# Three pads that move matmul operands by 64, 128 and 256 bytes in a one-core transformer kernel

## The chip, the cores and the metric

One Trainium2 chip, one of its cores. The metric is the device time of one launch in microseconds (us): the kernel is executed several times and the median stands for it.

## What is computed

The reference is two transformer blocks on 512 tokens of width 1024. What bears on the change are three large matrix products in the first block:

```python
q, k, v, z, gl = split_proj(h @ w_in[l])          # input products: h [512+256, 1024], w_in [1024, 7168]
...
act = gelu(einsum('td,thkd->thk', xb, u_tab[ib])) * gb     # PEER: 128 chosen experts of 16384 per token
out = einsum('thk,thkd->td', act, v_tab[ib])
```

The kernel computes the PEER part densely for three quarters of the tokens: the scores of all 16384 experts (keys `u`), a gate that is zero for those not chosen, and the sum over all values `v`. For the first 128 tokens it gathers the chosen rows instead.

## The kernel before

Every large product is done in split precision. An operand `a` of float32 is cut into `a_hi` (rounded to float32r by ScalarE) and `a_lo = a - a_hi` (VectorE or GpSimd), and a helper issues three matmuls of type float32r for each 128x128 block, at lines 100, 101 and 102:

```python
def product3(pe, out, left, right, start, stop):
    pe.matmul(out, left[0], right[0], start=start, stop=False)
    pe.matmul(out, left[0], right[1], start=False, stop=False)
    return pe.matmul(out, left[1], right[0], start=False, stop=stop)
```

The second argument of `pe.matmul` is the stationary operand (128 columns, loaded into the array by a LDWEIGHTS that the profile lists under PEld), the third the moving one (384 or 512 columns that stream through). In the profile's names the moving tile stands first and the stationary one second: `es_ob<-es_vh,es_ah` streams `es_vh` past `es_ah`. Each matmul has its own weight load, which runs while the matmul before it streams.

Three stages matter here, and in each TensorE follows one order without a break:

- Input products (`input_products`, `ip_` tiles, 57 to 477 us): 16 blocks of 512 output columns times 8 slices of the contraction. Stationary: token blocks of `ip_h_hi/lo` (later `ip_s_hi/lo`); moving: the weight slices `ip_wh`, `ip_wl` in a ring of 8. DMA brings a slice to `ip_raw`, ScalarE writes `ip_wh` (L652), GpSimd `ip_wl` (L728). 576 blocks, 1728 matmuls of 512 columns.
- Expert scores (`expert_scores`, `ex_` tiles, 855 to 1531 us): for each of 128 groups of keys and 8 slices, stationary `ex_uh`, `ex_ul` (made from `ex_u` by ScalarE L1559 and GpSimd L1684 or VectorE L1755), moving `wb_x_hi/lo`, 384 tokens. 3072 matmuls of 384 columns. `ex_u` is the same memory as `ex_room`, and is filled ahead of the stage.
- Expert sums (`expert_sums`, `es_` tiles, 1542 to 2069 us): for each of 128 groups of values, three token blocks by two halves. Stationary: the gated activations `es_ah`, `es_al` (made from `es_gated` at L2050, L2000, L2056); moving: the value rows `es_vh`, `es_vl`. 2304 matmuls of 512 columns.

Tiles are placed in SBUF in the order of their declaration, one behind the other, in each partition from byte 16,512 up. A tile in a `with` block of its own gives its room back, and a `hold` tile is never used: it only sets where the next one starts. Start bytes in a partition of the operands that this document speaks of, as the program places them (all strides inside these tiles are multiples of 512 bytes, so that the difference modulo 512 is the same for every matmul of a row):

| product | moving tile, start byte | stationary tile, start byte | moving minus stationary, modulo 512 |
|---|---|---|---|
| input products | ip_wh 147,584, ip_wl 163,968 | ip_h_hi 49,280, ip_h_lo 73,856 | 0 |
| expert scores | wb_x_hi 16,512, wb_x_lo 32,896 | ex_uh 149,632, ex_ul 166,016 | 0 |
| expert sums | es_vh 124,032, es_vl 140,416 | es_ah 162,944, es_al 169,088 | 0 |
| query product (mq, L100 to L102) | mq_ch 94,944, mq_cl 127,712 | wb_x_hi 16,512, wb_x_lo 32,896 | 96 |
| FFN up (pf_acc<-wb_x,pf_w) | wb_x_hi 16,512, wb_x_lo 32,896 | pf_wh 75,616, pf_wl 92,000 | 288 |
| FFN projection (pf_acc<-fo_p,wb_x) | fo_ph 165,728 / fo_pl 122,880 | wb_x_hi 16,512, wb_x_lo 32,896 | 224 for fo_ph, 384 for fo_pl |
| FFN down, half of the blocks (pf_acc<-pf_w,pf_h) | pf_wh 75,616, pf_wl 92,000 | pf_hh 120,672, pf_hl 165,728 | 0 |

Of the kernel before, what the change touches and what calls it, by code (L numbers as in the profile page):

```python
# [22 lines left out]
P = 128  # L23
# [11 lines left out]
KEPT_BASE = 102  # L35
LATENT_BASE = 106
DOWN_BASE = 215
DOWN_AT = 45600
SLICES_BASE = 205
GIVEN_BASE = 104  # L40
CARRIED_BASE = 200
# [34 lines left out]
def tensors(nc, ctx):  # L76
    def sb(name, shape, dt=F32):
        return ctx.enter_context(nc.sbuf_tensor(name, shape, dt, allow_name_mangling=True))

    def ps(name, shape, dt=F32):  # L80
        return ctx.enter_context(nc.psum_tensor(name, shape, dt, allow_name_mangling=True))

    return sb, ps
# [259 lines left out]
def input_products(nc, d, kept, kept_loaded):  # L343
# [17 lines left out]
    with phase(nc, "r0_loaded", "r1_loaded", "r2_loaded", "r3_loaded", "r4_loaded", "r5_loaded", "r6_loaded", "r7_loaded",  # L361
# [17 lines left out]
        sb, ps = tensors(nc, ctx)  # L379
# [15 lines left out]
            ada.append(early("ip_ada", [P, 2, KD, W]))  # L395
        z = sb("ip_z", [P, TT, 2 * D])
        raw = sb("ip_raw", [P, RING, W])
        wh = sb("ip_wh", [P, RING, W], F32R)
        wl = sb("ip_wl", [P, RING, W], F32R)
        stage = sb("ip_stage", [P, RING, W])  # L400
# [926 lines left out]
GR = 4  # L1327
GP = GT - 1
GI = 4
HOLD = 20736  # L1330
FIRST_BASE = 100
CARRIED_AT = 46688
GIVEN = KD * T + KD * 288 + 6 * KD + D
# [17 lines left out]
def expert_scores(nc, d, x, ut, ut_loaded, total, picked, weight, n_loaded, keyed, first):  # L1351
# [16 lines left out]
    with phase(nc, "u0_loaded", "u1_loaded", "u2_loaded", "u3_loaded", "u_hi", "u_lo", "h_done", "gelu_done",  # L1368
# [45 lines left out]
        sb, ps = tensors(nc, ctx)  # L1414
        hold = sb("ex_hold", [P, HOLD])
        uh = sb("ex_uh", [P, SLOTS, KD, NK], F32R)
# [451 lines left out]
def expert_sums(nc, d, total, picked, weight, n_loaded, keyed, ready, next_in, next_loaded, rows_stored):  # L1868
# [7 lines left out]
    with phase(nc, "e0_loaded", "e1_loaded", "v0_loaded", "v1_loaded", "v_hi", "v_lo", "gated", "act_hi", "act_lo", "key_done",  # L1876
# [5 lines left out]
        sb, ps = tensors(nc, ctx)  # L1882
        vt, ge, gk = keyed
        hold = sb("es_hold", [P, 2 * GI * (D + 2 * ND)])
        vh = sb("es_vh", [P, RING, D], F32R)
        vl = sb("es_vl", [P, RING, D], F32R)
        ag = sb("es_gated", [P, RING, ND])
        ah = sb("es_ah", [P, RING, ND], F32R)
        al = sb("es_al", [P, RING, ND], F32R)
# [1867 lines left out]
def whole_block(nc, d):  # L3757

    outer = ExitStack()
    with ExitStack() as ctx:  # L3760
        with ExitStack() as own:
            sb, _ = tensors(nc, own)
            given = (sb("ri_x", [P, KD, T]), sb("ri_low", [P, KD, 288]), sb("ri_mix", [P, 6, KD]), sb("jn_x0", [P, D]))
        with ExitStack() as own:
            sb, _ = tensors(nc, own)
            below = sb("wb_below", [P, 2 * KD * T])
            kept = (sb("at_q", [P, TT, D]), sb("at_k", [P, LK // P, D]), sb("at_ident", [P, P]))
        kept_loaded = [ctx.enter_context(nc.semaphore(f"{n}_kept", num=KEPT_BASE + i)) for i, n in enumerate(("keys", "queries"))]
        input_products(nc, d, kept, kept_loaded)
        x = split_pair(nc, ctx, "wb_x")  # L3770
        diff_attention(nc, d, x, kept, kept_loaded)
        with ExitStack() as own:
            sb, _ = tensors(nc, own)
            hold = sb("ex_before", [P, DOWN_AT - 2 * KD * T - 4128])
            keys_in = sb("ex_u", [P, 4, KD, NK])
        keys_loaded = ctx.enter_context(nc.semaphore("first_keys_loaded", num=DOWN_BASE))
        mix_and_query(nc, d, x, keys_in, keys_loaded)
        sb, _ = tensors(nc, ctx)
        total, picked, weight = sb("wb_po", [P, TT, D]), sb("wb_picked", [P, HK], U32), sb("wb_weight", [P, HK])
        with ExitStack() as own:  # L3780
            keyed = first_keys(nc, own)
        first = [ctx.enter_context(nc.semaphore(f"first_{n}_loaded", num=FIRST_BASE + i)) for i, n in enumerate(("gates", "values"))]
        given_loaded, rows_stored = [outer.enter_context(nc.semaphore(n, num=GIVEN_BASE + i)) for i, n in enumerate(("given_loaded", "x2_stored"))]
        expert_scores(nc, d, x, keys_in, keys_loaded, total, picked, weight, gather_semaphores(nc, ctx, "u", NR), keyed, first)
        expert_sums(nc, d, total, picked, weight, gather_semaphores(nc, ctx, "v", TT), keyed, first, given, given_loaded, rows_stored)
# [141 lines left out]
```

## Time and profile before

| | us |
|---|---|
| median of 3 runs | 3725.96 |
| lowest and highest run | 3718.17, 3726.2 |
| span of the profiled execution, first to last instruction | 3713.8 |
| TensorE busy in it | 3528.9 (95%) |
| VectorE / ScalarE / GpSimd busy | 2290.8 / 1476.7 / 1341.5 |

The profile gives its execution's own time as the span, 3713.8 us; the runs are timed from outside and lie 4.4 to 12.4 us above it. Matmuls are pipelined, and the duration that the profile gives one (389 ns for 512 columns) is longer than the time from its start to the next one's start. The rate of a stream of matmuls is therefore read in the timeline, from start to start; this distance is called the pitch here.

### The profile page before, as it was taken

How to read it: one execution, taken by the hardware profiler on the slowest of the kernel's cores; microseconds unless marked ns; L12 is line 12 of the kernel's file. 1: busy time of each engine (PE TensorE's matmuls, PEld its weight loads, DVE VectorE, ACT ScalarE, POOL GpSimd, SP SyncE). 2: the span in 40 equal slices, each digit the busy share in tenths (PEclk: the TensorE clock that was granted, in tenths of full speed). 3: DMA queues.
4: the chain of work that ended last, by engine and by line, in shares of the span. 5: the costliest groups of instructions: out<-in, count | busy, mean ns of one | idle time of the engine just before them, and what ended most of it. 6: DMA issues, size and time to landing. Idle time of an engine off the chain costs nothing. (4 is left out here: it accounts for less than half of the span.)

```text
span 3713.8 us, 58353 instructions
## 1 busy us (share of the span) xinstructions
PE 3528.9 (95%) x22109; PEld 2862.4 (77%) x22109; DVE 2290.8 (62%) x3622; ACT 1476.7 (40%) x2438; POOL 1341.5 (36%) x821
## 2 busy tenths in 40 slices
PE   8999988899998999899999899998999998989998
PEld 4777866788988999788888444897888864678887
DVE  5723167425999887688888866445566236646642
ACT  3312246334546996233333233223255214424540
POOL 3723400434776334454222011430334521413352
PEclk9999999999999999999999999999999997699999
DMA  7633410635678989999999335213333331032331
GB/s 273 228 101 113 168 48 1 238 128 168 220 224 274 323 318 342 361 369 364 357 349 360 105 115 169 80 32 119 90 100 91 113 132 69 1 115 81 100 113 57
DMA packets 367108, 651.14 MB, mean 175 GB/s; under 512 B 23944, under 2 KB 227592, under 8 KB 363716
## 3 DMA queue, kind: packets, MB, share of 16 engines
q1 hardware_dynamic: 321468, 475.37, 38.7%
q0 software_dynamic: 36864, 134.23, 9.7%
q10 hardware_dynamic: 8584, 38.89, 2.7%
q8 instruction: 132, 2.16, 0.2%
q14 instruction: 60, 0.49, 0.0%
HBM read 557.64 MB, written 96.00 MB: 176 GB/s over the span
## 5 line engine op out<-in xcount | busy, mean ns | idle before, releaser
L100 PE MATMUL ex_hb<-wb_x_hi,ex_uh 128*128 128x384 f32 x1024 | 350.8, 343 | 17.5 <-POOL ex_ul L1684 11.3
L101 PE MATMUL ex_hb<-wb_x_lo,ex_uh 128*128 128x384 f32 x1024 | 344.7, 337 | 0.0
L102 PE MATMUL ex_hb<-wb_x_hi,ex_ul 128*128 128x384 f32 x1024 | 344.5, 336 | 0.0
L100 PE MATMUL es_ob<-es_vh,es_ah 128*128 128x512 f32 x768 | 300.2, 391 | 11.8 <-DVE es_al L2056 11.8
L100 PE MATMUL pf_acc<-wb_x_hi,pf_wh 128*128 128x512 f32 (+2 forms) x768 | 298.3, 388 | 7.0 <-DVE wb_x_lo L2484 4.7
L101 PE MATMUL es_ob<-es_vl,es_ah 128*128 128x512 f32 x768 | 299.8, 390 | 0.0
L102 PE MATMUL es_ob<-es_vh,es_al 128*128 128x512 f32 x768 | 299.7, 390 | 0.0
L101 PE MATMUL pf_acc<-wb_x_lo,pf_wh 128*128 128x512 f32 (+2 forms) x768 | 297.7, 388 | 0.0
L102 PE MATMUL pf_acc<-wb_x_hi,pf_wl 128*128 128x512 f32 (+2 forms) x768 | 297.5, 387 | 0.0
L2035 POOL DMA_INDIRECT es_near<-in_peer_v,wb_picked x128 | 178.4, 1394 | 325.9 <-DVE wb_po L2059 320.6
L728 POOL TENSOR_TENSOR ip_wl<-ip_raw,ip_wh 128x512 fp32r<-128x512 f32 x128 | 190.8, 1499 | 226.8 <-ACT ip_wh L652 226.6
L1998 ACT ACTIVATE es_vh<-es_v 128x1024 fp32r<-128x1024 f32 x128 | 135.5, 1058 | 260.5 <-PE es_ob L102 170.7
L2054 DVE TENSOR_TENSOR es_vl<-es_v,es_vh 128x1024 fp32r<-128x1024 f32 x128 | 156.8, 1225 | 86.4 <-ACT es_vh L1998 86.3
L100 PEld LDWEIGHTS ex_hb<-wb_x_hi,ex_uh 128*128 128x128 f32 x1024 | 194.7, 190 | 19.7 <-POOL ex_ul L1684 12.5
L2519 DVE TENSOR_TENSOR pf_h<-pf_cv 128x512 f32<-128x512 f32 x44 | 174.5, 3965 | 50.3 <-ACT pf_cv L2395 50.2
L100 PE MATMUL ip_acc<-ip_wh,ip_h_hi 128*128 128x512 f32 x512 | 202.1, 395 | 0.9 <-DVE ip_s_lo L849 0.9
L101 PE MATMUL ip_acc<-ip_wl,ip_h_hi 128*128 128x512 f32 x512 | 201.3, 393 | 0.0
L102 PE MATMUL ip_acc<-ip_wh,ip_h_lo 128*128 128x512 f32 x512 | 201.1, 393 | 0.0
L652 ACT ACTIVATE ip_wh<-ip_raw 128x512 fp32r<-128x512 f32 x128 | 80.7, 632 | 290.2 <-PE ip_acc L102 241.8
L101 PEld LDWEIGHTS ex_hb<-wb_x_lo,ex_uh 128*128 128x128 f32 x1024 | 194.6, 190 | 0.0
L102 PEld LDWEIGHTS ex_hb<-wb_x_hi,ex_ul 128*128 128x128 f32 x1024 | 194.0, 190 | 0.0
L1684 POOL TENSOR_TENSOR ex_ul<-ex_u,ex_uh 128x1024 fp32r<-128x1024 f32 x62 | 164.5, 2671 | 70.9 <-ACT ex_uh L1559 68.4
(536 smaller groups left out, 8889.1 us busy)
## 6 DMA issues: line engine op xcount, KB each, us to landing
ex_u<-in_uT SPq DMA_DIRECT2D x128, 512.0 KB, 4.8
es_v<-in_peer_v SPq DMA_DIRECT2D x31, 2048.0 KB, 17.2
ip_raw<-in_w_in SPq DMA_DIRECT2D x112, 256.0 KB, 4.2
scratch_act<-ex_ge SPq DMA_DIRECT2D x128, 192.0 KB, 4.9
scratch_G<-eg_gates ACTq DMA_DIRECT2D x12, 2048.0 KB, 9.2
es_ge<-scratch_act SPq DMA_DIRECT2D x31, 768.0 KB, 6.2
es_g<-scratch_G SPq DMA_DIRECT2D x31, 768.0 KB, 10.1
fo_raw<-in_w_up SPq DMA_DIRECT2D x44, 512.0 KB, 5.3
```

Of the source, the lines that this page charges most:

```text
L100: pe.matmul(out, left[0], right[0], start=start, stop=False)
L101: pe.matmul(out, left[0], right[1], start=False, stop=False)
L102: return pe.matmul(out, left[1], right[0], start=False, stop=stop)
L652: act.activation(wh[:, n % RING], raw[:, n % RING], ACT.Copy).then_inc(w_hi, 1)
L728: pool.tensor_tensor(wl[:, n % RING], raw[:, n % RING], wh[:, n % RING].bitcast(F32), ALU.subtract).then_inc(w_lo, 1)
L1684: pool.tensor_tensor(ul[:, n % SLOTS], ut[:, n % SLOTS], uh[:, n % SLOTS].bitcast(F32), ALU.subtract).then_inc(u_lo, 1)
L1998: act.activation(vh[:, r], vt[:, m // GI, m % GI], ACT.Copy).then_inc(v_hi, 1)
L2035: pool.indirect_dma_start(near[:, n % RING], None, d["peer_v"], bass.IndirectOffsetOnAxis(ap=picked[:, n:n + 1], axis=0)).then_inc(n_loade ...
L2054: dve.tensor_tensor(vl[:, r], vt[:, u, c], vh[:, r].bitcast(F32), ALU.subtract).then_inc(v_lo, 1)
L2519: dve.tensor_tensor(h[:, u], cv[:, u, 0, :], cv[:, u, 1, :], ALU.mult).then_inc(h_done, 1)
```

## The change

Two pads are added and two constants grow by 32 elements:

```diff
-DOWN_AT = 45600
+DOWN_AT = 45632
...
         raw = sb("ip_raw", [P, RING, W])
+        shim = sb("ip_shim", [P, 64])
         wh = sb("ip_wh", [P, RING, W], F32R)
...
-HOLD = 20736
+HOLD = 20768
...
         vl = sb("es_vl", [P, RING, D], F32R)
+        shim = sb("es_shim", [P, 16])
         ag = sb("es_gated", [P, RING, ND])
```

`HOLD` sizes `ex_hold` (L1415), so `ex_uh` and all tiles declared behind it in `expert_scores` start 128 bytes later; `DOWN_AT` moves `ex_u` (L3774 and L3775) by the same 128 bytes, so that it still coincides with `ex_room`. `es_shim` moves `es_gated`, `es_ah`, `es_al` and what follows in `expert_sums` by 64 bytes. `ip_shim` moves `ip_wh`, `ip_wl`, `ip_stage` and what follows in `input_products` by 256 bytes. No pad is read or written, and no instruction, wait, transfer or size changes. Moving minus stationary, modulo 512, goes from 0 to 256 in the input products, to 384 in the expert scores and to 448 (that is -64) in the expert sums. All other products keep their differences.

## Rows read from the trace of the kernel before

**Rows 1.** Page, part 1: busy us (share of the span) xinstructions

```profile
PE 3528.9 (95%) x22109; PEld 2862.4 (77%) x22109; DVE 2290.8 (62%) x3622; ACT 1476.7 (40%) x2438; POOL 1341.5 (36%) x821
```

**Rows 2.** Stretches of the three stages: length, busy us (x) by engine, PEclk, DMA share, GB/s

```profile
57.40:477.00 419.60, 415.25 (x1793) 335.80 (x1792) 166.33 (x195) 106.32 (x173) 190.89 (x131) 0.99 0.48 160
...
855.60:1531.00 675.40, 651.58 (x4041) 648.38 (x4041) 581.50 (x1327) 418.40 (x846) 377.83 (x198) 0.98 0.81 282
...
1542.40:2069.00 526.60, 526.20 (x2313) 435.00 (x2314) 433.43 (x522) 192.60 (x261) 177.08 (x131) 1.00 0.98 352
```

**Rows 3.** TensorE's waits in those stretches: us in total, times, longest us

```profile
PE ex_hb L100 <- POOL ex_ul L1684: 11.3, 2, 9.0
...
PE es_ob L100 <- DVE es_al L2056: 11.8, 2, 11.4
```

**Rows 4.** Groups of instructions, shapes kept apart: busy us, mean ns, idle before

```profile
L100 PE MATMUL ex_hb<-wb_x_hi,ex_uh 128*128 128x384 f32 x1024 | 350.8, 343 | 17.5 <-POOL ex_ul L1684 11.3 <-DVE ex_ul L1721 6.3
...
L100 PE MATMUL es_ob<-es_vh,es_ah 128*128 128x512 f32 x768 | 300.2, 391 | 11.8 <-DVE es_al L2056 11.8
...
L100 PE MATMUL ip_acc<-ip_wh,ip_h_hi 128*128 128x512 f32 x512 | 202.1, 395 | 0.9 <-DVE ip_s_lo L849 0.9
...
L2678 PE MATMUL ri_acc<-ri_xm,ri_w 128*128 128x512 f32 x384 | 168.2, 594 | 0.0
```

**Rows 5.** Timeline of TensorE, difference 0: start us, duration us, instruction

```profile
400.08 0.39 PE L100 MATMUL ip_acc<-ip_wh,ip_h_hi 128*128 128x512 f32 x1
...
409.60 0.39 PE L100 MATMUL ip_acc<-ip_wh,ip_h_hi 128*128 128x512 f32 x1
...
925.05 0.33 PE L100 MATMUL ex_hb<-wb_x_hi,ex_uh 128*128 128x384 f32 x1
...
932.33 0.33 PE L100 MATMUL ex_hb<-wb_x_hi,ex_uh 128*128 128x384 f32 x1
...
1900.07 0.39 PE L100 MATMUL es_ob<-es_vh,es_ah 128*128 128x512 f32 x1
...
1909.59 0.39 PE L100 MATMUL es_ob<-es_vh,es_ah 128*128 128x512 f32 x1
...
2986.63 0.39 PE L100 MATMUL pf_acc<-pf_wh,pf_hh 128*128 128x512 f32 x1
...
2989.35 0.39 PE L100 MATMUL pf_acc<-pf_wh,pf_hh 128*128 128x512 f32 x1
```

**Rows 6.** Timeline of TensorE, other differences

```profile
760.14 0.39 PE L101 MATMUL mq_acc<-mq_cl,wb_x_hi 128*128 128x512 f32 x1
...
762.94 0.39 PE L101 MATMUL mq_acc<-mq_cl,wb_x_hi 128*128 128x512 f32 x1
...
2627.80 0.39 PE L100 MATMUL pf_acc<-fo_ph,wb_x_hi 128*128 128x512 f32 x1
...
2631.96 0.39 PE L100 MATMUL pf_acc<-fo_ph,wb_x_hi 128*128 128x512 f32 x1
...
2639.11 0.34 PE L100 MATMUL pf_acc<-wb_x_hi,pf_wh 128*128 128x384 f32 x1
...
2641.23 0.34 PE L100 MATMUL pf_acc<-wb_x_hi,pf_wh 128*128 128x384 f32 x1
...
2700.15 0.40 PE L100 MATMUL pf_acc<-wb_x_hi,pf_wh 128*128 128x512 f32 x1
...
2705.75 0.40 PE L100 MATMUL pf_acc<-wb_x_hi,pf_wh 128*128 128x512 f32 x1
```

**Rows 7.** Timeline of a plain float32 product, twelve matmuls merged

```profile
2199.50 5.31 PE L2678 MATMUL ri_acc<-ri_xm,ri_w 128*128 128x512 f32 x12
```

**Rows 8.** Groups of the other engines that read or write moved tiles

```profile
L728 POOL TENSOR_TENSOR ip_wl<-ip_raw,ip_wh 128x512 fp32r<-128x512 f32 x128 | 190.8, 1499 | 226.8 <-ACT ip_wh L652 226.6
...
L2050 DVE TENSOR_TENSOR es_gated<-es_ge,es_g 128x384 f32<-128x384 f32 x128 | 70.9, 554 | 1.8 <-SPq L1925 1.8
...
L2056 DVE TENSOR_TENSOR es_al<-es_gated,es_ah 128x384 fp32r<-128x384 f32 x128 | 70.8, 553 | 0.0
```

## The prediction

> **What bounds the kernel now.** The page comes first: TensorE is busy for 95% of the span, the next engine, VectorE, for 62% [rows 1]. An average does not say what a stage is worth, so the stretches of the three touched stages come second. In the input products TensorE is busy for 415.25 of 419.60 us, in the expert scores for 651.58 of 675.40 us, in the expert sums for 526.20 of 526.60 us [rows 2]; the largest waits there are 11.3 us for `ex_ul` and 11.8 us for `es_al`, two each, and nearly all of each is one stall at the start of its stage [rows 3]. The next engine has room in the first two (GpSimd 190.89 of 419.60 us, VectorE 581.50 of 675.40 us). So in all three the time is the number of matmuls times the pitch, and a nanosecond of pitch is paid 1728, 3072 and 2304 times. One thing limits a gain: in the expert sums the DMA engines are busy too, for 0.98 of the stretch at 352 GB/s, and in the scores for 0.81 [rows 2].
>
> The third view is the timeline, because durations mislead here: 391 ns [rows 4] is more than the distance between two starts. From 1900.07 to 1909.59 us stand 42 matmuls, 9.52 / 42 = 226.7 ns each; the input products give the same, 9.52 / 42 = 226.7 ns, and the 384-column scores (932.33 - 925.05) / 42 = 173.3 ns [rows 5]. At the full clock (2.4 GHz, granted at 0.98 to 1.00 in these stretches [rows 2]), 512 columns are 213.3 ns and 384 are 160.0 ns. So each pays 13.3 ns on top of its columns, 32 clock periods, whatever its length.
>
> **The change part by part.** Nothing is removed or added in work: no instruction, wait or DMA moves past another, and the order on every queue stays. All that changes is where tiles start. Its price can only come through a pitch, through an operation of another engine on a moved tile, or through a transfer to one.
>
> *How the pitch depends on the start bytes.* The kernel has products at other differences than 0, all float32r, all with one weight load for each matmul. At difference 96 (query product) 12 matmuls take 762.94 - 760.14 = 2.80 us, 233.3 ns each; at 288 (FFN up) 24 take 5.60 us, again 233.3 ns; for 384 columns at 288, 12 take 2.12 us, 176.7 ns [rows 6]. So the placement matters: 6.7 ns for 512 columns and 3.3 ns for 384. It is the difference and not the place, because FFN down at difference 0 has both of its tiles 32 bytes off the places of the three stages, and runs at 2.72 / 12 = 226.7 ns [rows 5].
>
> The FFN projection is the useful one. Its lines 100 and 102 stream `fo_ph` at difference 224, its line 101 streams `fo_pl` at 384, which is exactly what the expert scores get. 18 matmuls take 2631.96 - 2627.80 = 4.16 us, 231.1 ns each [rows 6]. If 224 costs what 96 and 288 cost, 233.3, the third is 3 x 231.1 - 2 x 233.3 = 226.7 ns: nothing beyond difference 0. What 96, 288 and 224 share is that they are odd multiples of 32; 0 and 384 are multiples of 64. All three new differences, 256, 384 and 448, are multiples of 64.
>
> *Expert scores, 128 bytes (new difference 384).* Taken at 0, from `fo_pl`. Bounds: 3072 x 3.3 ns = 10.2 us above, if it costs what 288 costs at 384 columns; below, if the 13.3 ns are a conflict that this placement removes. How much can be removed is read from a product whose columns stream at half the rate, twelve float32 matmuls in 5.31 us, the last with its mean duration of 594 ns [rows 4, 7]: (5.31 - 0.594) / 11 = 428.7 ns, 2 x 213.3 + 2.1. An overhead of 2.1 in place of 13.3 ns would give 3072 x 11.2 = 34.4 us back.
>
> *Input products, 256 bytes (new difference 256).* No row has 256. 96 and 288 differ by 192 and 0 and 384 by 128 (modulo 512), and within each pair the price is the same; a price that repeats at both steps repeats at 64, and one that repeats only every 128 (with 96 and 288, 32 to either side of a multiple, as mirror images) still gives 256 the price of 0. Taken at 0. Bounds: 1728 x 6.7 = 11.5 us above, 1728 x 11.2 = 19.4 us below.
>
> *Expert sums, 64 bytes (new difference 448).* This is the open one: 64 is where a price with a period of 64 and one with a period of 128 part, and no row shows an odd multiple of 64. With the shorter period it is 0. With the longer, it is unknown. Bounds: 2304 x 6.7 = 15.4 us above if it is like 32, twice that, 30.7 us, if the price grows with the distance; below, 2304 x 11.2 = 25.8 us by the pitch alone, but the DMA engines stand at 0.98 of 526.6 us, so that only 0.02 x 526.6 = 10.5 us can come out before the transfers are the bound. Taken at 0, since it is as near to 0 and 384 (whole multiples of 64) as a row gets.
>
> The SBUF page of the Trainium skill (SBUF — State Buffer, section Door 1) says that SBUF is read in 16-byte lines, with a penalty for crossing into a new line. All differences here, old and new, are whole numbers of such lines; by that rule no shift of 32, 64, 128 or 256 bytes would cost anything, and the sum would be 0 for all three stages. The sum above does not rest on it: the row at 96 bytes, six lines, shows 6.7 ns.
>
> *The other engines.* GpSimd's `ip_wl` reads one moved and one unmoved tile; with 190.8 us at 1499 ns each it is covered by the 419.60 us of its stage, and could double before TensorE waited [rows 2, 8]. In the expert sums VectorE reads unmoved tiles at L2050 (554 ns) and moved ones at L2056 (553 ns) of the same size; no difference to lose [rows 8]. If one arose, each ns costs 128 ns in a stage where VectorE has 526.60 - 433.43 = 93 us of room [rows 2]. Transfers keep their sizes; 0.
>
> *Sum.* 0 + 0 + 0: the span stays 3713.8 us, and the median 3725.96 us, 12.2 us above that span as now.
>
> **The rivals.**
>
> *The 64-byte shift is as bad as the 32-byte one (slower).* The place is the stream of `es_vh/es_vl` past `es_ah/es_al`; the price 15.4 us, 3741 us, or with a price that grows with the distance 30.7 us, 3757 us. For it: nothing in the trace has an odd multiple of 64, and the clean split of the rows is also that of a period of 128. Against: a period of 64 explains all rows with one term less. It decides from a pitch of 231.5 ns: 2304 x 4.9 = 11.2 us.
>
> *Every shift away from 0 costs (slower).* 10.2 + 11.5 + 15.4 = 37.1 us, 3763 us. For it: all three products at single other differences are slower. Against: the third matmul of the FFN projection works out at 226.7 ns.
>
> *The 13.3 ns are a conflict of equal starts (faster).* The weight load and the stream start on the same bytes modulo 512 now, and a shift takes them apart. Scores 34.4, input products 19.4, sums 10.5 us: 64.3 us if all three, 3662 us; the scores alone 3692, the input products alone 3707, the sums alone 3715 us. For it: 2.1 ns is what the float32 product shows. Against: no float32r stream in the trace runs below 226.7 ns, `fo_pl` at 384 included. The page TensorE: Matmul & The Clock Gate of the Trainium skill (sections Back-to-back issue gap, and Step-by-step) gives a pitch of N / 2.4 + 2.5 ns and two independent read ports, by which 512 columns would take 215.8 ns at any placement; the rows at 226.7 and 233.3 ns contradict it for these products, and by it the change would do nothing.
>
> **How the numbers follow.** About 0.3%, 11 us, is what a measurement of this kernel tells from no change. Forecast, no price anywhere: 0.54, with 3726 us; its own range is 3717 to 3735. The sums at 64 bytes cost: 0.17 (0.13 at 15.4 us, 0.04 at 30.7). Something in scores or input products costs too: 0.06. Scores, input products or both gain over 11 us: 0.19. The sums alone gain, at most 10.5 us: 0.04, within 0.3%. This makes faster 0.19, same 0.58, slower 0.23. The range leaves out the cases of several gains (under 3700) and those above 3748, some 0.17 together: 3700 to 3748.
>
> **What would show it.** In the timeline after: the pitch of `es_ob`, `ip_acc` and `ex_hb`, each over 42 matmuls, at 226.7, 226.7 and 173.3 ns, and durations of 389 and 334 ns. The first rival shows as 233 ns or more in `es_ob` with the other two unchanged; the second in all three; the third as a pitch towards 215 or 162 ns, with DMA share 1.00 and new waits on `es_v` or `es_al` in the sums. The prediction is wrong if the price repeats only every 128 bytes, or if equal starts are themselves what costs 13.3 ns.

## The result and the profile after

| | before | after |
|---|---|---|
| median, us | 3722.07 | 3736.86 |
| lowest and highest of 4 runs each | 3717.74, 3726.2 | 3727.38, 3742.77 |
| span of the profiled execution | 3713.8 | 3740.7 |

The ratio on record is 1.0044, with a 95% interval of 1.003 to 1.0058: the kernel became slower. The medians differ by 14.8 us, and the interval stands for 11 to 22 us. The profiled execution after is the slowest of the four. In every run that has both figures the time is 2.0 to 2.2 us above the span, so the profiled execution before took about 3716 us (an estimate), less than all four runs before. The two profiles thus differ by more than the medians do. Its span is 26.9 us longer; the stretches below are 28.0 us longer, and the rest 1.1 us shorter.

The page after, part 1, has the same numbers of instructions as [rows 1], and 32.1 us more of busy TensorE:

```profile
PE 3561.0 (95%) x22109; PEld 2881.8 (77%) x22109; DVE 2297.9 (61%) x3622; ACT 1476.2 (39%) x2438; POOL 1328.4 (36%) x821
```

The stretches of the three stages after, with the columns of [rows 2], and as the fourth the first stretch of FFN up matmuls with 128 columns:

```profile
57.40:477.00 419.60, 414.69 (x1792) 335.32 (x1791) 167.89 (x195) 106.31 (x173) 192.60 (x131) 0.99 0.47 160
855.30:1536.40 681.10, 660.13 (x4041) 657.80 (x4041) 584.32 (x1327) 418.43 (x845) 380.00 (x198) 0.98 0.80 279
1547.10:2088.60 541.50, 540.07 (x2312) 434.90 (x2313) 434.68 (x522) 191.69 (x261) 159.84 (x131) 1.00 0.96 342
2676.90:2697.50 20.60, 20.58 (x97) 20.58 (x97) 7.34 (x7) 7.85 (x8) 4.54 (x1) 0.50 0.07 19
```

The same last stretch in the kernel before:

```profile
2657.40:2670.60 13.20, 10.98 (x97) 10.85 (x97) 5.75 (x5) 6.56 (x6) 4.53 (x1) 1.00 0.00 1
```

Against [rows 2] the input products take what they took, the scores 681.10 - 675.40 = 5.7 us more and the sums 541.50 - 526.60 = 14.9 us more. The last stretch takes 7.4 us more for another reason: the granted clock is 0.50 of 2.4 GHz in it, the lower level, where it was 1.00. In both executions TensorE waited 2.4 us for `wb_x_lo` just ahead of it. The single execution profiled of the kernel with the 64 bytes alone has this too, and so has that of the level kernel, which leaves the three stages alone (both below); those with the 128 or the 256 bytes alone don't. So it follows none of the pads; why it comes is not known.

The waits of TensorE after, with the columns of [rows 3], did not grow, so no wait made the stages longer:

```profile
PE es_ob L100 <- DVE es_al L2058: 11.8, 2, 10.4
PE ex_hb L100 <- POOL ex_ul L1685: 8.9, 2, 8.1
```

In the groups after, by shape, the durations of the scores rise by 4 ns and those of the sums by 6 ns; the input products stay at 395 [rows 4]:

```profile
L100 PE MATMUL ex_hb<-wb_x_hi,ex_uh 128*128 128x384 f32 x1024 | 355.0, 347 | 15.2 <-POOL ex_ul L1685 8.9 <-DVE ex_ul L1722 6.3
...
L100 PE MATMUL es_ob<-es_vh,es_ah 128*128 128x512 f32 x768 | 304.8, 397 | 11.8 <-DVE es_al L2058 11.8
...
L100 PE MATMUL ip_acc<-ip_wh,ip_h_hi 128*128 128x512 f32 x512 | 202.1, 395 | 0.9 <-DVE ip_s_lo L850 0.9
```

The timeline of TensorE after gives the pitches:

```profile
400.12 0.39 PE L100 MATMUL ip_acc<-ip_wh,ip_h_hi 128*128 128x512 f32 x1
...
409.64 0.39 PE L100 MATMUL ip_acc<-ip_wh,ip_h_hi 128*128 128x512 f32 x1
...
999.81 0.34 PE L100 MATMUL ex_hb<-wb_x_hi,ex_uh 128*128 128x384 f32 x1
...
1009.85 0.34 PE L100 MATMUL ex_hb<-wb_x_hi,ex_uh 128*128 128x384 f32 x1
...
1899.61 0.40 PE L100 MATMUL es_ob<-es_vh,es_ah 128*128 128x512 f32 x1
...
1909.41 0.40 PE L100 MATMUL es_ob<-es_vh,es_ah 128*128 128x512 f32 x1
```

Input products: 42 matmuls in 9.52 us, 226.7 ns, as before. Scores: 57 in 10.04 us, 176.1 ns, where [rows 5] give 173.3. Sums: 42 in 9.80 us, 233.3 ns, where they give 226.7. Priced by count: the sums 2304 x 6.7 = 15.4 us (14.9 in the stretch), the scores 3072 x 2.8 = 8.6 us, of which 17.5 - 15.2 = 2.3 us came back as shorter waits for `ex_ul`, which leaves 6.3 (5.7 in the stretch).

### The profile page after: what moved, and what is told of

Read it like the earlier page. It is cut to its first block and busy times, and to the rows that moved or that the text cites. A ratio compares the mean times of both kernels' runs of the same rounds, so it can differ in the third digit from the quotient of the medians.

```text
span 3740.7 us, 58353 instructions
## 1 busy us (share of the span) xinstructions
PE 3561.0 (95%) x22109; PEld 2881.8 (77%) x22109; DVE 2297.9 (61%) x3622; ACT 1476.2 (39%) x2438; POOL 1328.4 (36%) x821
## 5 line engine op out<-in xcount | busy, mean ns | idle before, releaser
L100 PE MATMUL ex_hb<-wb_x_hi,ex_uh 128*128 128x384 f32 x1024 | 355.0, 347 | 15.2 <-POOL ex_ul L1685 8.9
L2037 POOL DMA_INDIRECT es_near<-in_peer_v,wb_picked x128 | 161.2, 1259 | 357.2 <-DVE wb_po L2061 351.0
```

What stands on the lines that cost most here:

```text
L2037: pool.indirect_dma_start(near[:, n % RING], None, d["peer_v"], bass.IndirectOffsetOnAxis(ap=picked[:, n:n + 1], axis=0)).then_inc(n_loade ...
```

## The experiments

In what follows a pitch with two decimals is a mean over starts in the timeline, over all unbroken streams of the product (over 1,400 matmuls in each of the three stages). Six kernels were run once each, beside one run of the kernel before. Single runs of the kernel before spread by 16 us (27 runs, 3709.72 to 3725.88), so there the pitch carries the verdict and not the time.

### One part at a time

The 64 bytes alone:

```diff
+        shim = sb("es_shim", [P, 16])
```

> Only the 64-byte pad of the expert sums. Theory A (each stage pays the pitch that its own difference gives, and nothing else moves): the pitch of es_ob is 233.3 ns as in the changed kernel, the other two stages keep 173.3 and 226.7 ns, and the kernel is 2304 x 6.67 ns = 15.4 us slower, 0.41%. Theory B (the loss comes from the changed kernel as a whole, for instance from clock stretches that fall elsewhere): the pitch is 233.3 ns but the median moves by less than 5 us.

Measured: 3735.33 us (10 runs) against 3720.74 (27 runs), ratio 1.0041 (1.0027 to 1.0054), 14.6 us. Its timeline has 45 matmuls in 10.50 us, 233.3 ns, and its stretches of the sums and of the scores are 541.60 and 673.70 us:

```profile
1899.25 0.39 PE L100 MATMUL es_ob<-es_vh,es_ah 128*128 128x512 f32 x1
...
1909.75 0.40 PE L100 MATMUL es_ob<-es_vh,es_ah 128*128 128x512 f32 x1
```

```profile
1540.40:2082.00 541.60, 540.84 (x2312) 435.59 (x2313) 434.79 (x522) 191.57 (x261) 156.24 (x131) 1.00 0.96 342
855.30:1529.00 673.70, 651.34 (x4041) 648.19 (x4041) 580.76 (x1327) 418.33 (x845) 376.57 (x198) 0.98 0.81 282
```

The 64 bytes cost what the prediction's first rival said, in the stage where it said it; in the scores they cost nothing.

The 128 bytes alone:

```diff
-DOWN_AT = 45600
+DOWN_AT = 45632
...
-HOLD = 20736
+HOLD = 20768
```

> Only the 128-byte shift of the expert scores. Theory A: the pitch of ex_hb is 176.0 ns where no gate matmul stands between, and the kernel is 3072 x 2.67 ns = 8.2 us slower, 0.22%. Theory B: the shift is free by itself, pitch 173.3 ns, and the 176 ns came from a neighbouring cause; no change in time.

Measured: 3726.84 us (12 runs), ratio 1.0018 (1.0008 to 1.0028), 6.1 us. The pitch of the scores is 57 matmuls in 10.04 us, 176.1 ns, that of the sums 226.67 ns:

```profile
999.93 0.34 PE L100 MATMUL ex_hb<-wb_x_hi,ex_uh 128*128 128x384 f32 x1
...
1009.97 0.34 PE L100 MATMUL ex_hb<-wb_x_hi,ex_uh 128*128 128x384 f32 x1
```

```profile
853.60:1535.10 681.50, 660.39 (x4041) 657.93 (x4041) 583.10 (x1328) 419.11 (x845) 380.00 (x198) 0.98 0.80 279
```

So the 128 bytes are not free: a small cost, below the 11 us that the prediction took as what a measurement can tell, but real here (the interval excludes 1).

The 256 bytes alone:

```diff
+        shim = sb("ip_shim", [P, 64])
```

> Only the 256-byte pad of the input products. Both theories: pitch of ip_acc 226.7 ns, no change in time, within 2 us of before. A pitch over 227 ns, or a time over 6 us longer, would mean that the pad costs through something else than the pitch.

Measured: 3721.61 us (12 runs), ratio 1.0004 (0.9994 to 1.0014), pitch 226.67 ns. No cost can be told. The three parts add to 14.6 + 6.1 + 0.9 = 21.6 us; the change as a whole measured 14.8, with an interval that ends at 22, so they agree only just. By the pitches alone the sum is 15.4 + 6.3 = 21.7 us.

### The differences taken away

If the difference sets the pitch, products that had one of 96, 224, 288 or 384 before must gain when brought to 0 or 256. This kernel keeps the three stages as before and moves the others:

```diff
+        shim = sb("mq_shim", [P, 40])
...
-        hold = sb(f"{name}_hold_a", [P, 18400])
+        hold = sb(f"{name}_hold_a", [P, 18432])
...
-        hold = sb(f"{name}_hold_b", [P, 2520])
+        hold = sb(f"{name}_hold_b", [P, 2496])
...
+        shim = sb("pf_shim", [P, 8])
```

> The three stages as before; instead the products that stand at odd multiples of 32 bytes are moved so that their differences become 0 or 256 modulo 512: a pad of 160 bytes in mix_and_query, one of 32 bytes in projected_ffn, and the slices fo_pl/fo_ph moved by 128 and 32 bytes. Theory A: 233.3 becomes 226.7 ns in the query and output products, in FFN up and FFN down, 231.1 becomes 226.7 ns in the FFN projections. 768 + 1920 + 480 matmuls x 6.67 ns + 384 x 4.4 ns = 22.8 us faster, 3700 us against 3723. Theory B (the price belongs to certain tiles or stages, not to the difference): the pitches stay and so does the time.

Measured: 3700.37 us (6 runs), ratio 0.9947 (0.9931 to 0.9964), 20.4 us faster than before (the 22.8 us expected lie inside the interval) and 36 us faster than after. Its timeline, against [rows 6]:

```profile
762.07 0.39 PE L100 MATMUL mq_acc<-mq_ch,wb_x_hi 128*128 128x512 f32 x1
...
765.47 0.39 PE L100 MATMUL mq_acc<-mq_ch,wb_x_hi 128*128 128x512 f32 x1
...
2622.25 0.39 PE L100 MATMUL pf_acc<-fo_ph,wb_x_hi 128*128 128x512 f32 x1
...
2626.33 0.39 PE L100 MATMUL pf_acc<-fo_ph,wb_x_hi 128*128 128x512 f32 x1
...
2640.17 0.33 PE L100 MATMUL pf_acc<-wb_x_hi,pf_wh 128*128 128x384 f32 x1
...
2642.77 0.33 PE L100 MATMUL pf_acc<-wb_x_hi,pf_wh 128*128 128x384 f32 x1
...
2700.07 0.39 PE L100 MATMUL pf_acc<-wb_x_hi,pf_wh 128*128 128x512 f32 x1
...
2705.51 0.39 PE L100 MATMUL pf_acc<-wb_x_hi,pf_wh 128*128 128x512 f32 x1
```

The query product goes from 233.3 to 3.40 / 15 = 226.7 ns, the FFN projection from 231.1 to 4.08 / 18 = 226.7, FFN up from 176.7 to 2.60 / 15 = 173.3 and from 233.3 to 5.44 / 24 = 226.7. This is the cause turned round: no instruction is saved, and the time becomes shorter.

### What a shift costs by its size

Pads in elements of 4 bytes; the difference is given with its sign in the table further on. The first two:

```diff
+        shim = sb("ip_shim", [P, 32])
...
-DOWN_AT = 45600
+DOWN_AT = 45616
-HOLD = 20736
+HOLD = 20752
...
+        shim = sb("es_shim", [P, 32])
```

> Moving minus stationary modulo 512: input products 128, scores 448 (64 bytes), sums 384 (128 bytes, what fo_pl has). Theory A (the price depends on the difference modulo 256 and only 0 is free): pitch 233.3 ns in the input products and in the sums, about 176 ns in the scores. Theory B (128 is cheap for 512 columns, as the FFN projection's 231.1 ns suggested): 226.7 ns or little more in the input products and the sums, and 176 ns in the scores, where 384 columns make the difference.

Measured: 3753.03 us against 3722.41; pitches 232.38 (input products), 174.97 (scores), 233.33 ns (sums).

The other has `ip_shim` [P, 16], `HOLD` 20800 with `DOWN_AT` 45664, and `es_shim` [P, 64].

> Differences: input products 64, scores 256, sums 256. Both theories: scores 173.3 ns and sums 226.7 ns, since 256 was free in the input products. Theory A: input products 233.3 ns, as the sums had at minus 64; a sign that mattered would show as another pitch here. If 256 is free only in the input products, scores and sums show 176 and 233 ns.

Measured: 3722.22 us against 3722.41; 228.89, 173.4, 226.67 ns. For the input products, 42 matmuls in 9.62 us:

```profile
400.06 0.39 PE L100 MATMUL ip_acc<-ip_wh,ip_h_hi 128*128 128x512 f32 x1
...
409.68 0.39 PE L100 MATMUL ip_acc<-ip_wh,ip_h_hi 128*128 128x512 f32 x1
```

Offsets below 64 bytes need one tile that holds both halves of an operand, shown for the sums (the same is done for `ip_wh`, `ip_wl` and for `ex_uh`, `ex_ul`):

```diff
-        ah = sb("es_ah", [P, RING, ND], F32R)
-        al = sb("es_al", [P, RING, ND], F32R)
+        both = sb("es_a", [P, 2 * RING * ND + 16], F32R)
+        ah, al = (both[:, 4 + u * RING * ND:4 + (u + 1) * RING * ND].rearrange("p (r n) -> p r n", r=RING) for u in range(2))
```

> Differences of 16 bytes in all three stages (input products 16, scores and sums minus 16), made inside one tile. Theory A: any difference other than a multiple of 256 costs, so 233.3, 176 to 177 and 233.3 ns. Theory C (the 13.3 ns that every stream still pays are a conflict that a shift smaller than 32 bytes removes): pitches below 226.7 and 173.3 ns, down to 215 and 162 ns.

Measured: 3738.5 us against 3722.41; 231.67, 174.4, 233.33 ns. For the input products, 42 matmuls in 9.73 us:

```profile
400.11 0.40 PE L100 MATMUL ip_acc<-ip_w,ip_h_hi 128*128 128x512 f32 x1
...
409.84 0.39 PE L100 MATMUL ip_acc<-ip_w,ip_h_hi 128*128 128x512 f32 x1
```

The same with other offsets: 12 elements (48 bytes) in the input products, 2 (8 bytes) in the scores, 1 (4 bytes) in the sums.

> Differences: input products 48, scores minus 4, sums minus 8 bytes. Theory A: 233.3, 176 to 177, 233.3 ns. Theory D (only the 32-byte or 64-byte unit counts, offsets inside it are free): 233.3 ns at 48, and 173.3 and 226.7 ns at 4 and 8. Theory C: below 226.7 or 173.3 ns somewhere.

The expectation has two offsets exchanged: it says 4 bytes for the scores and 8 for the sums. By the edit the scores had -8 and the sums -4 bytes.

Measured: 3738.19 us against 3722.41; 233.33, 173.38, 232.38 ns.

In this run and the one before it the time rose by 16 us, where the pitches come to more: 1728 x 5.0 + 3072 x 1.1 + 2304 x 6.7 = 27 us with 16 bytes, and 1728 x 6.7 + 2304 x 5.7 = 25 us here. Part of the second gap shows in the trace: TensorE waited 3.0 us for GpSimd's part of the score weights (here `ex_w`, the tile that holds `ex_ul`) where it waited 11.3 us before [rows 3]. The rest can be the spread of single runs.

### The step on the FFN projection

The prediction split 231.1 ns into two matmuls at 233.3 and one at 226.7. Here the projection of the first FFN has both halves at 224, that of the second both at 384, and the stages get +192, +128 and +128:

```diff
+        shim = sb("ip_shim", [P, 48])
...
+        shim = sb("es_shim", [P, 96])
...
+        hold = sb(f"{name}_hold_a", [P, 18488 if name == "fo" else 18400])
...
+        hold = sb(f"{name}_hold_b", [P, 2432 if name == "fo" else 2560])
...
+        hold = sb(f"{name}_hold_c", [P, 3072 if name == "fo" else 3032])
```

with `HOLD` 20832 and `DOWN_AT` 45696.

> Tests the step of the prediction that split 231.1 ns of the FFN projection into two prices. In the first projection (fo) both slices now stand at difference 224, in the second (fs) both at 384; the first block's stages get 192 (input products), 128 (scores) and 128 (sums). Theory P (the prediction's step: each matmul pays for its own difference): 233.3 ns in fo, 226.7 ns in fs. Theory E (the price belongs to the whole cycle of matmuls and does not add up): anything but that pair; by the sums at 384 it should be 233.3 ns in fs. For the sign: if the price depends on the difference modulo 256 alone, the sums at 128 and the scores at 128 repeat 233.3 and 176.0 ns, which they showed at 384.

Measured: 3742.91 us against 3722.12; 233.33 (input products, +192), 176.06 (scores, +128), 232.38 (sums, +128), 233.33 ns (projection at 224) and 232.33 ns (projection at 384). Of the one at 224, 57 matmuls in 13.30 us:

```profile
2626.67 0.40 PE L100 MATMUL pf_acc<-fo_ph,wb_x_hi 128*128 128x512 f32 x1
...
2639.97 0.40 PE L100 MATMUL pf_acc<-fo_ph,wb_x_hi 128*128 128x512 f32 x1
```

Both alone are slower than the two mixed.

One stream in this kernel says that the difference is not all that sets a pitch. FFN up with 384 columns stands at 288 in both FFNs of every kernel here but the level one. Its two streams of 96 matmuls run at 176.7 ns in each of these eleven kernels, 2.12 / 12 in [rows 6], with one exception: in the second FFN of this kernel 93 matmuls take 16.12 us, 173.3 ns.

```profile
3350.41 0.34 PE L100 MATMUL pf_acc<-wb_x_hi,pf_wh 128*128 128x384 f32 x1
...
3366.53 0.33 PE L100 MATMUL pf_acc<-wb_x_hi,pf_wh 128*128 128x384 f32 x1
```

Neither of its operands was moved; in that FFN only the projection ahead of it was. Why this stream is faster is not known.

The last one gives the opposite sign: `ip_shim` [P, 8], `HOLD` 20848 with `DOWN_AT` 45712, `es_shim` [P, 112], so that the sums have +64 where the change gave them -64.

> Differences: input products 32, scores 64, sums 64. Theory F (which operand stands ahead matters, a stage does not): the sums at plus 64 repeat the 228.9 ns of the input products at plus 64, not the 233.3 ns of minus 64. Theory G (the stage's order of tiles matters, the sign does not): the sums stay at 233.3 ns. Input products at 32: 233.3 ns in both, as FFN up at 288.

Measured: 3736.64 us against 3722.12; 233.33 (input products, +32), 173.38 (scores, +64), 228.89 ns (sums, +64). In the sums, 42 matmuls in 9.61 us:

```profile
1899.85 0.39 PE L100 MATMUL es_ob<-es_vh,es_ah 128*128 128x512 f32 x1
...
1909.46 0.39 PE L100 MATMUL es_ob<-es_vh,es_ah 128*128 128x512 f32 x1
```

### All differences together

Moving minus stationary start in bytes, modulo 512, and the mean pitch in ns:

| difference | 512 columns | where |
|---|---|---|
| 0 | 226.67 | the three stages before; level |
| 256 | 226.67 | input products after; sums with 256; level |
| -4, -16 | 232.38, 233.33 | sums |
| +16, +32, +48 | 231.67, 233.33, 233.33 | input products |
| +64 | 228.89 | input products, and sums |
| -64 | 233.33 | sums after |
| +128 | 232.38 | input products, and sums |
| -128 | 233.33 and 232.33 | sums, and FFN projection |
| 96, 192, 224, 288 | 233.33 | query product, input products, FFN projection, FFN up |

| difference | 384 columns |
|---|---|
| 0, 256, +64, -8 | 173.33 to 173.4 |
| -16, -64 | 174.4, 174.97 |
| +128, -128 | 176.06, 176.1 |
| 288 | 176.67 (one stream of 22 at 173.33) |

The entries for -16 and -64 at 384 columns are means over streams that run at different levels; see the last section.

## Why the prediction was wrong in two stages and right in one

The forecast was 3726 us with a range of its own of 3717 to 3735. The measured 3736.86 us lie above that, and above the four runs before. They lie inside the wide range, 3700 to 3748, only because it was drawn to take in the rivals; the mechanism of the forecast, no price anywhere, did not hold. The prediction also put the median 12.2 us above the span "as now". That is no property of the kernel: the time of each run is 2.0 to 2.2 us above its own span, and the profile was of a faster execution.

*What bounds the kernel.* Right. The cost is pitch times count: the stretches grew by 14.9 us for 15.4, and by 5.7 us for 8.6 less 2.3 of wait; no wait grew.

*Input products at 0.* Right: 226.67 ns, 1.0004. But the number was luck: the argument for it, that a price repeats every 64 or every 128 bytes, was wrong, since 64, 128 and 192 all cost. 256 is free by its own measurement.

*Expert sums at 0.* This is the step that failed, with the most us: "Taken at 0, since it is as near to 0 and 384 (whole multiples of 64) as a row gets." Measured 14.6 us alone, 233.33 ns; the first rival, with its price of 15.4 us and its sign of 233 ns in `es_ob`, came true. The step leaned on 384 being free, which it is not. The price does not grow with the distance: no stage's pitch was above 233.33 ns, which was the upper bound taken from the rows at 96 and 288.

*Expert scores at 0, from the FFN projection.* Failed too: "the third is 3 x 231.1 - 2 x 233.3 = 226.7 ns". The arithmetic was right, but the model under it was not: it gave each matmul a price of its own, whatever its neighbours are, and that of 384 came out as nothing. At 224 alone the pitch is 233.33, at 384 alone 232.33, and mixed two to one 231.1, lower than either. Measured in the scores 6.1 us, within the bound of 10.2.

*The second rival, every shift costs, 37.1 us.* Fell as a whole (256 is free), and holds for two of its three parts.

*The third rival, 13.3 ns as a conflict of equal starts.* Fell. Its sum needed pitches below 226.67 or 173.33 ns, and no mean pitch above is below. Equal starts are the best placement tried, with 256 beside it. Where the 13.3 ns come from stays open. The formula of the Trainium skill that the prediction set against this rival, N / 2.4 + 2.5 ns, is called the gap of an isolated matmul in that section (TensorE: Matmul & The Clock Gate, section Back-to-back issue gap); for a stream of pairs of a weight load and a matmul the same section gives about 131 ns at 512 columns. These float32r streams are such pairs and ran at 226.67 ns at best, so neither figure fits them.

*Other engines and transfers at 0.* Held. In the sums the DMA share fell from 0.98 to 0.96 with the same bytes in a longer stage; the transfers had no part in the cost.

*The chances.* The forecast had 0.54 and the first rival 0.17. For it stood only that both 384 and a period of 64 pointed one way, and both rested on one mixed row. The rows had given one clean statement: both differences other than 0 that stood alone in a product, 96 and 288, cost 6.7 ns at 512 columns. This should have weighed more than a split of a mean.

What stays open: the mechanism. That the weight load of the next matmul and the stream of this one get in each other's way at their reads is argued only from the fact that the relative place, and not the place, sets the pitch; no run shows the reads. The records of the weight loads don't show it either. In the sums they last 189 ns before and 188 ns after, while the pitch grew by 6.7 ns (before first, then after; TensorE's weight loads by shape, in the columns of [rows 4]):

```profile
L100 PEld LDWEIGHTS es_ob<-es_vh,es_ah 128*128 128x128 f32 x768 | 144.8, 189 | 43.0 <-DVE es_al L2056 12.9
L100 PEld LDWEIGHTS es_ob<-es_vh,es_ah 128*128 128x128 f32 x768 | 144.8, 188 | 47.4 <-DVE es_al L2058 12.6
```

Nor is it known why +64 costs 2.2 ns and -64 costs 6.7.

## What to carry to other kernels

Where a matmul of float32r has its own weight load, try the moving and the stationary operand at the same start byte modulo 256 (differences of 0 and 256 modulo 512 are what was measured, in one kernel on one core), then read the pitch of each such product in the timeline from start to start. The step from 226.7 to 233.3 ns for 512 columns is 3% of that product, for no work at all. A pad ahead of any tile moves all tiles behind it, so check every pair again after it. Don't take the price of one matmul out of the mean of a mixed stream; run that placement alone.

## What the runs showed of the hardware that was not expected

- Only differences of 0 and 256 of those tried give the lowest pitch seen for 512 columns, 226.67 ns. Four bytes cost 5.7 ns (232.38), sixteen 5.0 to 6.7 ns. The Trainium skill (SBUF — State Buffer, section Door 1) speaks of 16-byte lines and a penalty for crossing into a new one. By that rule a shift by whole lines changes nothing; the rows at 16, 64 and 128 bytes contradict it as an account of this pitch.
- The sign counts, and the stage doesn't: +64 gives 228.89 ns in the input products and in the sums, -64 gives 233.33 in the sums.
- 384 columns are less sensitive: +64 and -8 bytes cost nothing, and the most seen is 3.3 ns, half of that of 512 columns.
- One difference can run at several levels. In the kernel with 16-byte offsets the unbroken streams of the scores have either 173.33 or 176.67 ns each, with few between; at -64 they have 173.3, about 174.8 or 176.7 ns, most of them the last. At -128 the sums have 233.33 and the FFN projection 232.33.
- A pitch can outlast its difference. In the kernel before, FFN down changes from a stream at 288 to one at 0 (the half in the table of start bytes). The first eight steps at difference 0 take 1.85 us, 231 ns each, and only then come 226.7 ns. In the level kernel, where the stream ahead stands at 256, the first eight take 226.8 ns each in ten of the twelve such streams of both FFNs. The prediction's row for FFN down, from 2986.63 us on, lies behind such eight steps; its tiles stand at 352 modulo 512 and those of the three stages at 128, 224 bytes apart and not 32. From the kernel before:

```profile
2940.35 0.40 PE L100 MATMUL pf_acc<-pf_wh,pf_hh 128*128 128x512 f32 x1
...
2942.20 0.39 PE L102 MATMUL pf_acc<-pf_wh,pf_hl 128*128 128x512 f32 x1
```

- The same section of the skill that the prediction cited for two independent read ports (TensorE: Matmul & The Clock Gate, section Step-by-step) says that loading the next weights takes nothing from the running matmul. A pitch that depends on the relative place of the two operands, by up to 6.7 ns, is not what one expects from that for float32r, and the runs decide on the pitch. Which part of the sentence fails is not shown, as no run shows the reads.
